# Layer 1's per-head mean squares from high and low parts in two single-pass products, one unit later

## The reference

```python
def differential_attention(h, w_in, ..., subln, w_out, cos, sin, lambda_init):
    ...
        p = jax.nn.softmax(sc, axis=-1)
        a = p[:, :, 0] - lam * p[:, :, 1]
        return jnp.einsum('bhqk,bkhe->bqhe', a.astype(v.dtype), v)
    o = from_blocks(lax.map(block, (to_blocks(q), jnp.arange(s // QBLK))))
    o = rms_norm(o, subln) * (1.0 - lambda_init)
    return o.reshape(b, s, B_HEADS * 2 * HEAD_DIM) @ w_out
```

## Time and profile before

| | |
|---|---|
| time, median of 3 executions | 1149.14 us (1148.43 to 1151.99) |
| profiled execution | 1147.77 us, its span 1146.0 us |
| mean granted TensorE clock | 0.999 of full speed |
| TensorE busy | 1133.8 us (99%), 5688 products |
| VectorE busy | 694.5 us (61%) |
| ScalarE busy | 466.0 us (41%) |
| GpSimd busy | 5.1 us |
| transfers | 101.94 MB, on average 89 GB/s |

### The profile page before, as it was taken

How to read it: one execution, slowest core, us unless ns; L and a number is a source line. 1 busy time by engine, 2 the same in 40 slices (tenths; PEclk the granted TensorE clock), 3 DMA queues, 4 the chain that set the end, 5 groups by cost and what they waited for, 6 DMA issues and landing times.

```text
span 1146.0 us, 15943 instructions
## 1 busy us (share of the span) xinstructions
PE 1133.8 (99%) x5688; PEld 964.9 (84%) x5688; DVE 694.5 (61%) x1173; ACT 466.0 (41%) x943; POOL 5.1 (0%) x32
## 2 busy tenths in 40 slices
PE   9999999999999999999999999999999999999997
PEld 8999888888888878889998899688888888888886
DVE  6888775565565543338677777847565565643334
ACT  7788553222122132327455656544122222223224
POOL 1000000000000000000000000000000000000000
PEclk9999999999999999999999999999999999999999
DMA  7220043323323123234121111033333233122232
GB/s 233 72 82 29 9 141 110 108 75 110 97 86 110 55 76 108 92 124 148 49 84 57 56 55 55 16 112 112 92 92 110 79 104 110 56 72 92 92 101 101
DMA packets 144523, 101.94 MB, mean 89 GB/s; under 512 B 12041, under 2 KB 137190, under 8 KB 144486
## 3 DMA queue, kind: packets, MB, share of 16 engines
q1 hardware_dynamic: 144462, 101.45, 28.6%
q10 hardware_dynamic: 24, 0.01, 0.0%
HBM read 99.34 MB, written 2.10 MB: 89 GB/s over the span
## 4 chain that ended last, share of the span: by engine, by line
PE 93%; DVE 4%; ACT 1%; issue 1%; DMA 0%; SPq 0%; DVEq 0%; ACTq 0%
PE ps L550 23%; PE ps L552 22%; PE ps L551 22%; PE ps L620 17%; PE ps L661 3%; PE ps L848 2%; PE ps L874 1%; DVE w_lo L1555 1%; PE ps L723 1%; PE ps L925 1%; DVE h_lo L1586 1%; ACT w_hi L1142 0%; DMA raw<-in_a_w_in 0%; PE ps L879 0%; DVE ssacc L1580 0%
## 5 line engine op out<-in xcount | busy, mean ns | idle before, releaser
L1142 ACT ACTIVATE w_hi<-raw 128x512 fp32r<-128x512 f32 (+2 forms) x204 | 191.5, 970 | 295.5 <-PE ps L552 294.6
L550 PE MATMUL ps<-h_hi,w_lo 128*128 128x512 f32 x704 | 274.7, 390 | 0.0
L552 PE MATMUL ps<-h_hi,w_hi 128*128 128x512 f32 x704 | 273.9, 389 | 0.0
L551 PE MATMUL ps<-h_lo,w_hi 128*128 128x512 f32 x704 | 273.9, 389 | 0.0
L1555 DVE TENSOR_TENSOR w_lo<-raw,w_hi 128x512 fp32r<-128x512 f32 (+2 forms) x204 | 222.6, 1113 | 11.9 <-ACT w_hi L1142 11.9
L551 PEld LDWEIGHTS ps<-h_lo,w_hi 128*128 128x128 f32 x704 | 132.2, 188 | 27.9 <-issue 0.5
L550 PEld LDWEIGHTS ps<-h_hi,w_lo 128*128 128x128 f32 x704 | 132.2, 188 | 27.8 <-issue 0.5
L552 PEld LDWEIGHTS ps<-h_hi,w_hi 128*128 128x128 f32 x704 | 132.2, 188 | 27.3
L1945 DVE TENSOR_TENSOR normed<-ps,rstd 128x512 f32<-128x512 f32 x44 | 30.4, 692 | 169.0 <-PE ps L552 161.6
L620 PE MATMUL ps<-w_hi,h_hi 128*128 128x384 f32 x368 | 126.7, 344 | 0.0
L620 PE MATMUL ps<-w_hi,h_lo 128*128 128x384 f32 x368 | 125.6, 341 | 0.5 <-DVE w_lo L1555 0.5
(11 more groups left out here) (207 smaller groups left out, 1606.9 us busy)
## 6 DMA issues: line engine op xcount, KB each, us to landing
raw<-in_ffn_w_up SPq DMA_DIRECT2D x88, 512.0 KB, 4.6
raw<-in_ffn_w_down SPq DMA_DIRECT2D x44, 512.0 KB, 3.2
raw<-in_b_w_in SPq DMA_DIRECT2D x24, 512.0 KB, 4.9
raw<-in_a_w_in SPq DMA_DIRECT2D x3, 1024.0 KB, 7.4
raw<-in_a_w_out SPq DMA_DIRECT2D x2, 1536.0 KB, 7.0
raw<-in_b_w_out SPq DMA_DIRECT2D x2, 1536.0 KB, 6.3
x_tok<-in_x SPq DMA_DIRECT2D x4, 512.0 KB, 4.3
out<-x_tok SPq DMA_DIRECT2D x8, 256.0 KB, 2.0
```

Of the source, the lines that this page charges most:

```text
L550: pe.matmul(out_, a_lo, b_hi, start=start, stop=False)
L551: pe.matmul(out_, a_hi, b_lo, start=False, stop=False)
L552: return pe.matmul(out_, a_hi, b_hi, start=False, stop=stop)
L1142: act.activation(w_hi[:, s, at], raw[:, s, at], ACT.Copy).then_inc(hi_done, 1)
```

## The change

The full float32 product of ones and squares is replaced by two float32r products, of the low part and of the high part of the squares. ScalarE makes the high part right after the square (a copy of 128x512), VectorE the low part at the end of the unit (a subtraction of 128x512). The ones matrix is the same memory, of type float32r, which the other users read as float32. TensorE issues the two products in the next unit, between the second and third slab after `probs_b(u, 0)` (in unit 7 after the first slab); those of unit 7 itself stand where the old product stood. In the next unit ScalarE does `exps_b(u, 1)` ahead of `rsqrt_head` and one slice of weights ahead of `high_out_b`; VectorE does `combine_b(u, 1)` ahead of `norm_head` and one slice of weights ahead of `low_out_b`.

```diff
+            def mean_square_head(u, bank):
+
+                pe.wait_ge(osqlo_done, u + 1)
+                pe.matmul(ps[:, bank, :], ones_r[:, :], osq_lo[:, :], start=True, stop=False)
+                pe.matmul(ps[:, bank, :], ones_r[:, :], osq_hi[:, :], start=False, stop=True)\
+                  .then_inc(oms_done, 1)
+
             def unit_b(u, s, more=True, more2=True):
...
                 probs_b(u, 0)
-                run(slabs, n[0])
+                run(slabs, n[0] - 2)
+                if not (isinstance(u, int) and u == 0):
+                    mean_square_head(u - 1, TB)
+                run(slabs, 2)
                 scores_b(u, 2)
...
                 run(slabs, n[8])
-
-                pe.wait_ge(osq_done, u + 1)
-                pe.matmul(ps[:, TB if more else LAST_MS, :], ones_d[:, :], osq[:, :], start=True, stop=True)\
-                  .then_inc(oms_done, 1)
+                if not more:
+                    mean_square_head(u, LAST_MS)
                 run(slabs, 24)
...
                 high_p("B", u, 0)
+                exps_b(u, 1)
                 if before:
                     rsqrt_head(u - 1)
-                exps_b(u, 1)
                 if more:
                     take("B", u + 1, 1 - s, 1)
+                weights(0)
                 if before:
                     high_out_b(u - 1)
-                weights(0)
                 weights(1)
...
                 act.activation(sq[:, 0, :], ps[:, OBK, :], ACT.Square).then_inc(osq_done, 1)
+                act.wait_ge(osq_done, u + 1)
+                act.activation(osq_hi[:, :], sq[:, 0, :], ACT.Copy).then_inc(osqhi_done, 1)
                 if more2:
                     take("B", u + 2, s, 0)
...
+            def low_square(u):
+                dve.wait_ge(osqhi_done, u + 1)
+                dve.tensor_tensor(osq_lo[:, :], sq[:, 0, :], osq_hi[:, :].bitcast(F32),
+                                  ALU.subtract).then_inc(osqlo_done, 1)
...
                 low_p("B", u, 0)
+                combine_b(u, 1)
                 if before:
                     norm_head(u - 1)
-                combine_b(u, 1)
                 if more:
                     low_v("B", u + 1, 1 - s, 1)
+                weights(0)
                 if before:
                     low_out_b(u - 1)
-                weights(0)
                 maxima_b(u, 2)
...
                 if more2:
                     low_v("B", u + 2, s, 0)
+                low_square(u)
```

More of the change, by code:

```diff
@@ L121, in trunk @@
         ident = sb("ident", [P, P])
-        ones_d = sb("ones_d", [P, P])
+        ones_r = sb("ones_r", [P, P], F32R)
+        ones_d = ones_r[:, :].bitcast(F32)
         mask_q = sb("mask_q", [P, P], BF16)
@@ L173, in trunk @@
             prob = sb("prob", [P, 2, 1024], F32, st)
+            osq_hi = sb("osq_hi", [P, T], F32R, st)
+            osq_lo = sb("osq_lo", [P, T], F32R, st)
         with ExitStack() as st:
@@ L264, in trunk @@
         osq_done = sem("osq_done")
+        osqhi_done = sem("osqhi_done")
+        osqlo_done = sem("osqlo_done")
         oms_done = sem("oms_done")
@@ L527, in _ @@
                 pool.memset(invf[:, i:i + 1], inv_freq(i)).then_inc(const_done, 1)
-            pool.memset(ones_d[:, :], 1.0 / D).then_inc(const_done, 1)
+            pool.memset(ones_d, 1.0 / D).then_inc(const_done, 1)
             pool.memset(eps[:, :], EPS).then_inc(const_done, 1)
@@ L585, in mean_square @@
                 pe.wait_ge(ss_done, KC * norm)
-                pe.matmul(ps[:, TB, :], ones_d[:, :], ssacc[:, :], start=True, stop=True)\
+                pe.matmul(ps[:, TB, :], ones_d, ssacc[:, :], start=True, stop=True)\
                   .then_inc(ms_done, 1)
@@ L993, in out_projection @@
                             out_products(l, dc, rows)
-            osq = sq[:, 0, :]
             start_unit0("A")
```

## The result

| | before | changed |
|---|---|---|
| median on the same chip | 1148.8 us (10 runs) | 1152.05 us (10 runs, 1151.77 to 1153.24) |
| ratio, 95% interval | | 1.0026 [1.0016, 1.0036] |
| profiled execution, span | 1147.77, 1146.0 us | 1152.11, 1150.3 us |

A forecast was written before the change was run, and what follows sets the result against it. TensorE's own stream was taken to bound the kernel (93% of the span). Six boundaries +3.5, unit 6 to 7 -0.6 and unit 7's pair +0.5 sum to +3.4 us: 1152.5 us, eight in ten between 1149.2 and 1155.2.

The forecast's parts named there:

- The removed product covered a wait: Before tile 2's first product: the 0.85 us product supplied 0.4 us of spare time for tile 0's values' low part.
- The copy pushes the take: ScalarE, six boundaries: copy between square and take of tile 0; values' low part until 578.06, TensorE's product at 578.11.
- 0.12 us for the hole, 0.46 for the pair: Six boundaries: tile 2's first product 0.12 us later, plus the pair's 0.46: +0.58 us each, +3.5 us in all.
- Spare times: Steady units: the pair has 0.8 us to spare, tile 3 has 1.2 us for tile 1's low part.
- Unit 6 to 7: No take here; VectorE's row maxima come sooner, TensorE's wait shrinks from 1.24 to about 0.35 us: -0.6 us.
- The 0.1 us for a first product after a hole: Pair at unit 6 to 7: a first product after a hole takes about 0.1 us more.
- Unit 7's own pair: End of unit 7: square, copy, subtraction, then pair from 752.35; second product at 753.14 instead of 752.61: +0.5 us.
- The gain arrives: Rival: tile 0's low part isn't what stops TensorE; -2.4 us, 1146.7 us; chance 0.08.
- A second hole: Rival: later mean square delays tile 1's take beyond tile 3's start, 0.5 us in six units; +6.4 us, 1155.5; chance 0.08.
- Only the spare time is lost: Rival: copy overlaps the take, row maxima still decide the low part's start; +0.4 us, 1149.5 us; chance 0.10.
- The cheaper pair: Rival: the pair's products take 0.13 us each, not 0.23; +1.8 us, 1150.9 us; chance 0.02.

The follow-up runs named there:

- the full product at the new place: Changed kernel with the full float32 product of the squares at the new place, without copy and subtraction: 1150.47 us against 1148.36, ratio 1.0017.
- the single product at the old place: Kernel before with one float32r product replacing the full one, low part of the squares left out: 1145.18 us against 1148.36, ratio 0.9969.
- the take first: Changed kernel with tile 0's take ahead of ScalarE's square and its low part ahead of VectorE's row maxima: 1145.85 us against 1148.36, ratio 0.9977.
- The order alone: Kernel before with only the four exchanges of steps on ScalarE and VectorE: 1147.58 us against 1148.6, ratio 0.9992.

## Why the forecast was right

**Direction, size and cause** were right: +3.4 us forecast, +3.0 (1.8 to 4.1) measured, +3.8 in the trace of the attention. The times can't tell 3.0, 3.4 and 3.8 apart; the trace can, and by it the sum was 0.4 us too low. By its own steps:

- *The removed product covered a wait.* Shown by the full product at the new place (+1.9 us from the move) and by the single product at the old place, whose gain was cut by the same wait.
- *The copy pushes the take.* Forecast: low part until 578.06, TensorE at 578.11, in the clock of the kernel before; in the changed kernel all is 0.55 us later, from the square on: 578.60 and 578.66. Shown by moving the copy (-0.44 to -0.49 us each) and by doubling it (+0.63 to +0.69 each).
- *0.12 us for the hole, 0.46 for the pair.* The hole is exact. The pair's term was mis-sized by 0.05: +0.58 forecast, +0.60 to +0.67 measured, mean 0.63. It isn't in the pair, which takes 0.46 to 0.47 us. With the take first, from the transpose at 602.49 to the scores at 605.99 it is 3.50 us; before, from 603.50 to 606.49, it is 2.99 us: 0.51 for a pair of 0.46. The changed kernel has the same 0.51 behind its hole: from the waiting product to the scores 3.47 us (604.80 to 608.27), before 2.96 (603.53 to 606.49). With the hole's 0.12 that makes the 0.63. More of the projection's products around the pair follow at 0.18 instead of 0.17 us. The moved full product shows about as much: by its rows the move should cost 577.70 - 577.19 - 0.03 = 0.48 us of hole, the boundaries have 0.51 to 0.56. Why this is so stays open.
- *Spare times.* The pair of steady heads never waits: the low part of the squares ends at 579.20, the pair starts at 580.15, 0.95 us (forecast 0.8). Tile 3 doesn't wait either. VectorE's low part of tile 1 ends at 583.21, tile 3 starts at 584.42, 1.2 us (forecast 1.2):

```profile
582.87 0.34 DVE L1621 SCALAR_TENSOR_TENSOR v_lo<-ps,vecs,v_hi 128x128 fp32r<-128x128 f32 x1
...
584.42 0.33 PE L625 MATMUL ps<-w_hi,h_lo 128*128 128x384 f32 x1
```

- *Unit 6 to 7.* Total -0.57 us, forecast -0.6. The pair starts 2.18 us after the square, as worked out (728.40 to 730.58), and VectorE's row maxima come 0.56 us sooner against the square (forecast 0.58). But the remaining wait was forecast at 0.35 us and is 0.63. TensorE leaves the place 0.32 us later, as said, and yet is only 0.07 us late at the last product ahead of the waiting transposes (10.39 us behind the square, before 10.32). The step that failed is the silent one that a delay is handed on unchanged. The kernel before had a short wait on the way, ahead of the values of tile 1, which only its weight load shows:

```profile
737.03 0.19 PEld L874 LDWEIGHTS ps<-pt_hi,v_lo 128*128 128x128 f32 x1 [0.45 <-DVE pt_lo L1642]
```

  There the first product of the values starts 0.41 us after the one ahead of it (736.62 to 737.03), in the changed kernel 0.23 (741.33 to 741.56). TensorE's delay was taken up there and just behind it. The total stands, since VectorE sets when the wait ends. The order alone shows it too: there VectorE is ahead and the wait ahead of these values is gone (736.66 to 736.89, 0.23 us).

  The 0.1 us for a first product after a hole was right in size by luck. The rows it was read from, 577.99 to 578.25, have no hole ahead of them, only the transpose. Behind the real hole it is 0.33 us instead of 0.23 (734.93 to 735.26).
- *Unit 7's own pair.* +0.55 us, forecast +0.5: it starts 2.04 us after the square, forecast 2.03.

**The rivals.** (1) *The gain arrives* fell: the low part ends at 578.60, 0.9 us behind the start of TensorE's transpose. The rule of the Trainium skill on the engine with the highest occupancy (page "Perfetto Trace Analysis", section "Identifying the Most-Contended Engine") picks the right engine here, TensorE at 99%. Taken alone it speaks for a gain, and the trace does not agree; the run with the take first shows what that section leaves out, the next wait in line. (2) *A second hole* fell, by the rows at 582.87 and 584.42. (3) *Only the spare time is lost* fell: VectorE had finished its maxima and stood 0.39 us idle for the values' high part (row at 578.25). It is close to the truth once the copy is behind the take, +0.6 us where it had +0.4. (4) *The cheaper pair* fell: 0.23 us from L890 to L891. The Trainium skill, page "TensorE: Matmul & The Clock Gate", section "Back-to-back issue gap", gives about 131 ns for a matmul of 512 columns in a sustained stream; the trace does not agree.

## What to carry to other kernels

A shorter instruction on the bounding engine gains its time only if the next instruction that waits has that much time to spare: look for it in the timeline ahead of the edit, and make room there first. A helper step that a cheaper form needs (here a copy) belongs behind whatever the bounding engine waits for next, not where its input happens to be ready. And a form that pays in the middle of a pipeline can lose at its end, where nothing covers its preparation; keep the old one there.

## What the runs showed that had not been expected

- A wait of TensorE stands shorter on the product than on its weight load, by an amount that differs from place to place: 0.3 us at the boundaries (0.73 and 1.03 us at 578.66, 0.24 and 0.54 at 577.70 in the moved full product), 0.13 us ahead of the transposes at 743.99 (0.63 and 0.76), 0.44 us ahead of the pair at 734.93 (0.62 and 1.06). A shorter wait shows on the load alone: the single product's six waits of together 2.3 us, and the 0.45 us wait at 737.03 of the kernel before. Spare time is read from the distance of two starts, or from the weight loads.
- The first product behind a hole takes about 0.1 us more until the next one starts, for holes of 0.5 to 1.7 us alike: 0.28 or 0.29 instead of 0.17 us with 384 columns (578.66 to 578.94; 0.29 with the moved full product and with the copy doubled), 0.34 instead of 0.23 with 512 (756.14 to 756.48). But at the boundaries the hole isn't the cause of most of it: behind the transpose the first product takes 0.26 us without any hole too (577.99 to 578.25 before, 577.32 to 577.58 with the take first). There the hole adds 0.02 or 0.03 us. Behind a product of 512 columns, at 756.14, it adds the whole 0.11.
- A pair of 512 columns put among products of 384 cost 0.05 us beyond its own 0.46, as told above.
